# Sample attention over cached rows: block turns on VectorE, contractions of 32 on 16 tiles of TensorE, rotary keys loaded as stored

## The reference

```python
def sample_attention(q_lat, q_rope, c_kv, k_rope, cache_ckv, cache_krope, page_table):
    ...                                # m0, l0, acc0 from the new tokens
    def step(carry, pages):
        m, l, acc = carry
        ck = cache_ckv[pages]          # 128 rows x 256
        kr = cache_krope[pages]        # 128 rows x 64
        s = mla_scores(q_lat, q_rope, ck, kr)      # q_lat.ck + q_rope.kr
        m_new = jnp.maximum(m, jnp.max(s, axis=-1))
        alpha = jnp.exp(m - m_new)
        p = jnp.exp(s - m_new[..., None])
        l = l * alpha + jnp.sum(p, axis=-1)
        acc = acc * alpha[..., None] + jnp.einsum('bhqk,bkc->bqhc', p, ck, ...)
        return (m_new, l, acc), None
```

## Time and profile before

| | us | share of the span |
|---|---|---|
| span | 1993.0 | |
| TensorE matmuls (PE) | 1818.9 | 91% |
| TensorE weight loads (PEld) | 1240.8 | 62% |
| VectorE (DVE) | 751.0 | 38% |
| ScalarE (ACT) | 453.6 | 23% |
| GpSimd (POOL) | 318.3 | 16% |

### The profile page before, as it was taken

The page is one execution under the profiler, slowest core; times in us unless marked ns, Lnnn a source line. Parts: engine busy times, 40 slices in busy tenths (PEclk is TensorE's granted clock), DMA queues, the critical chain, the costliest instruction groups (busy, mean ns, idle before and its releaser), DMA issues.

```text
span 1993.0 us, 28968 instructions
## 1 busy us (share of the span) xinstructions
PE 1818.9 (91%) x11420; PEld 1240.8 (62%) x11420; DVE 751.0 (38%) x1684; ACT 453.6 (23%) x999; POOL 318.3 (16%) x437
## 2 busy tenths in 40 slices
PE   7999999999979999999999997999698888898884
PEld 5677888888845655656666664655465565565551
DVE  3343334444423434334554554576322311111116
ACT  3122211111113323223443443222110101111013
POOL 1034311111110000001111112333411211111100
PEclk9999999999989999999999997999698998998997
DMA  6112215555620000027999984545699999999986
GB/s 209 56 66 76 76 56 212 211 213 212 223 86 1 1 1 1 1 64 219 308 293 301 306 292 173 184 137 179 255 415 415 417 415 406 413 397 396 415 326 262
DMA packets 107021, 432.89 MB, mean 217 GB/s; under 512 B 25216, under 2 KB 30752, under 8 KB 77184
## 3 DMA queue, kind: packets, MB, share of 16 engines
q1 hardware_dynamic: 86704, 330.02, 44.2%
q0 software_dynamic: 20160, 101.24, 14.8%
q10 hardware_dynamic: 48, 0.13, 0.0%
HBM read 388.12 MB, written 63.66 MB: 227 GB/s over the span
## 4 chain that ended last, share of the span: by engine, by line
PE 33%; DMA 17%; DVE 2%; issue 1%; SPq 1%; ACT 1%; POOL 0%; POOLq 0%; DVEq 0%; ACTq 0%; PEldq 0%
DMA arena<-in_w_up_dram 16%; PE psum L1414 8%; PE psum L1158 6%; PE psum L1288 6%; PE psum L1169 4%; PE psum L1185 3%; PE psum L1271 1%; PE psum L1176 1%; SPq L802 1%; DMA arena<-in_w_down_dram 1%; PE psum L1313 1%; PE psum L1433 1%; DMA arena<-y_rows 0%; DVE arena L2547 0%; PE psum L1278 0%
## 5 line engine op out<-in xcount | busy, mean ns | idle before, releaser
L931 PE MATMUL psum<-arena 128*128 128x256 f32 x1792 | 394.0, 380 | 2.0 <-DVE arena L2116 2.0
L931 PEld LDWEIGHTS psum<-arena 128*128 128x128 f32 x1792 | 338.7, 190 | 55.7 <-issue 5.4
L1414 PE MATMUL psum<-arena 128*64 128x256 f32 (+1 forms) x2048 | 286.8, 414 | 65.7 <-DMA arena<-in_w_up_dram 63.9
L1414 PEld LDWEIGHTS psum<-arena 128*64 128x64 f32 (+1 forms) x2048 | 203.3, 156 | 139.3 <-issue 80.1
L2494 DVE TENSOR_TENSOR arena<-arena,psum 128x256 f32<-128x256 f32 x36 | 15.2, 423 | 314.4 <-ACT arena L1716 314.4
L1433 PE MATMUL psum<-arena 128*64 128x512 f32 (+1 forms) x512 | 131.3, 595 | 2.7 <-DMA arena<-in_w_down_dram 2.7
L1158 PEld LDWEIGHTS psum<-arena 128*128 128x128 f32 x1024 | 113.7, 142 | 29.5 <-issue 27.9
L1158 PE MATMUL psum<-arena 128*128 128x128 f32 x1024 | 127.3, 277 | 0.0
L1288 PE MATMUL psum<-arena 128*128 128x512 f32 x256 | 115.2, 603 | 1.3 <-ACT arena L1649 1.3
L1614 ACT COPY arena<-psum 128x512 f32<-128x512 f32 x128 | 72.0, 588 | 171.6 <-PE psum L1158 171.6
L1931 POOL DMA_INDIRECT y_rows<-arena x36 | 40.4, 1123 | 407.3 <-DVE arena L2503 407.3
(11 more groups left out here) (337 smaller groups left out, 2273.0 us busy)
## 6 DMA issues: line engine op xcount, KB each, us to landing
arena<-in_w_gate_dram SPq DMA_DIRECT2D x64, 1024.0 KB, 11.8
arena<-in_w_up_dram SPq DMA_DIRECT2D x64, 1024.0 KB, 20.2
arena<-in_w_down_dram SPq DMA_DIRECT2D x64, 1024.0 KB, 22.0
arena<-in_w_in_dram SPq DMA_DIRECT2D x8, 2048.0 KB, 10.9
z_act<-arena SPq DMA_DIRECT2D x64, 256.0 KB, 2.1
rope_turned<-arena SPq DMA_DIRECT2D x32, 512.0 KB, 4.8
arena<-rope_turned SPq DMA_DIRECT2D x64, 256.0 KB, 9.1
arena<-z_act SPq DMA_DIRECT2D x8, 2048.0 KB, 7.9
```

The lines of the kernel that those rows point to most:

```text
L931: last = mm(out[:, 0:256], x[:, k, :], w[:, k, :], start=(k == 0), stop=(k == 3))
L1414: last = mm(bank(2 + u)[rows, DE * x:DE * x + DE], xg_t[u][:, k, rows], w_e[slot][x][:, k, :], start=(k == 0), stop=(k == KD - 1))
```

## The change

VectorE turns each chunk as it lies, in blocks of 32x32, with two instructions of 128x2048 (turn_keys), straight from ck[q] into a flat tile ck_f; TensorE's turns, their copies on ScalarE and VectorE and the tile ck_t are gone. A block of 32 partitions of ck_f then holds 32 of the 256 latent values of the rows of its own 32 partitions, so the score contracts over 32 at a time: ten steps (eight latent, two rotary), for four row tiles a and four column tiles j, 160 calls with 128 columns each. Row tile a writes bank a; the scores of a chunk lie in four banks, a quarter of each, two chunks side by side. The queries are spread to all four groups of partitions by 24 small DMAs during the attention of the prompt (q_rep, qr_rep) and copied for each sequence on VectorE. The rotary keys are read with one DMA of 512 KB in pieces of 4 KB, as they lie in rope_turned, into two places; the load for n waits for the score of n - 2.

VectorE's round for chunk n: maximum, its two small steps, the additions of chunk n - 1 (in the last chunk of four those of chunk n too, at the end), the turns of chunk n + 2. In the last round of four the copies of the next queries stand ahead of the maximum. Chunk 0 is turned within the last units of the prompt's attention, chunk 1 ahead of the loop. TensorE's order: turn_probs n, score n + 1, weigh n. The loads of z wait for the weighing of chunk 29, w_o for that of chunk 30 (before: z for 28 and 29, w_o for 30 and 31).

```diff
             def rope_load(n):
-                if n >= 4:
-                    sp.wait_ge(c_s, n - 3)
-                sp.wait_ge(rk_mv[n % 2], 16 * PRE + 32 * (n // 2))
-                keys = rope_t[P * n:P * n + P, :].rearrange("(a f) (c m) -> c f a m", a=4, c=2)
-                for c in range(2):
-                    sp.dma_start(rope_home(n)[32 * c:32 * c + 32, :].rearrange("f (a m) -> f a m", a=4),
-                                 keys[c]).then_inc(rk_mv[n % 2], 16)
+                if n >= 2:
+                    sp.wait_ge(c_s, n - 1)
+                sp.wait_ge(rk_mv[n % 2], 16 * PRE + 16 * (n // 2))
+                sp.dma_start(kr_f[n % 2].rearrange("p c m -> p (c m)"), rope_t[P * n:P * n + P, :]).then_inc(rk_mv[n % 2], 16)
...
+            rope_load(0)
+            for u in range(2):
+                sp.wait_ge(b_ev[u], groups_done(sched, ("sL", 3))[u])
+            for a in range(4):
+                rows = slice(32 * a, 32 * a + 32)
+                for f in range(4):
+                    sp.dma_start(q_rep[rows, :, f, :], qs[32 * f:32 * f + 32, :, :]).then_inc(qrep_in, 16)
+                for f in range(2):
+                    sp.dma_start(qr_rep[rows, f, :], qsr[32 * f:32 * f + 32, :]).then_inc(qrep_in, 16)
             sp.wait_ge(ends, 8)
+            rope_load(1)
...
+            def score(n, q):
+
+                for f in (8, 9, *range(8)):
+                    for a in range(4):
+                        rows = slice(32 * a, 32 * a + 32)
+                        for j in range(4):
+                            keys = kr_f[q % 2][rows, f - 8, P * j:P * j + P] if f >= 8 else ck_f[q % 2][f // 4][rows, f % 4, 4 * j:4 * j + 4, :]
+                            last = mm(scores_at(q)[RS * j:RS * j + RS, a, :], q_now[rows, f, :], keys, start=(f == 8), stop=(f == 7))
                 last.then_inc(c_s, 1)
...
                     if more:
-                        pe.wait_ge(c_in[(q + 1) % 4], 16 * i + (16 if q < 3 else 32) + (16 * PRE if (q + 1) % 4 < 2 else 0))
-                        turn(n + 1, (q + 1) % 4, range(6))
+                        score_inputs(n + 1, (q + 1) % 4, 2 * i + (q + 1) // 2 + 1)
+                        if q == 3:
+                            pe.wait_ge(q_ready, i + 2)
                     turn_probs(n)
                     if more:
-                        turn(n + 1, (q + 1) % 4, range(6, NU))
+                        score(n + 1, (q + 1) % 4)
                     weigh(n, q)
-                    if more:
-                        if q == 3:
-                            pe.wait_ge(q_ready, i + 2)
-                        score(n + 1, (q + 1) % 4, 2 * i + (q + 1) // 2 + 1)
...
+            def turn_keys(q, half):
+                V.transpose(ck_f[q % 2][half].rearrange("p f r i -> p r f i"),
+                            ck[q][:, :, P * half:P * half + P].rearrange("p r (f k) -> p r f k", f=4)).then_inc(c_tr, 1)
+
             for what, n in late_units:
                 unit(what, n)
+                if (what, n) in (("PV", NTP * H // 2 - 3), ("PV", NTP * H // 2 - 2)):
+                    dve.wait_ge(c_in[0], 16 * PRE + 16)
+                    turn_keys(0, n - NTP * H // 2 + 3)
...
                     dve.wait_ge(c_s, n + 1)
-                    ch(red(m_part, bank(5), AX.X, ALU.max))
+                    if q == 3 and not last_batch:
+
+                        now = bass.ds(RS * i + RS, RS)
+                        for c in range(2):
+                            ts(q_now[:, 4 * c:4 * c + 4, :], q_rep[:, c, :, now], 1.0, None, ALU.mult)
+                        ts(q_now[:, 8:10, :], qr_rep[:, :, now], 1.0, None, ALU.mult).then_inc(q_ready, 1)
+                    ch(red(m_part, scores_at(q), AX.XY, ALU.max))
...
+                    if q:
+                        add_chunk(n - 1, (q - 1) % 2)
+                    if q < 2 or not last_batch:
+                        dve.wait_ge(c_in[(q + 2) % 4], 16 * i + (16 if q < 2 else 32) + (0 if q < 2 else 16 * PRE))
+                        for half in range(2):
+                            turn_keys((q + 2) % 4, half)
+                    if q == 3:
+                        if last_batch:
+                            dve.wait_ge(uv_in, 32)
+                            v_norm(0, 0)
+                        add_chunk(n, 1)
```

More of the change, by code:

```diff
@@ L1148, in _, with score_inputs @@
             last.then_inc(n_pe, 1)
[L1149 to L1170 removed]
+            def score_inputs(n, q, loads):
+                pe.wait_ge(rk_mv[q % 2], 16 * PRE + 16 * loads)
+                pe.wait_ge(c_tr, 2 * n + 2)
+            def score(n, q):
[5 more added lines that the diff above has]
+                            last = mm(scores_at(q)[RS * j:RS * j + RS, a, :], q_now[rows, f, :], keys, start=(f == 8), stop=(f == 7))
                 last.then_inc(c_s, 1)
@@ L1187, in weigh @@
                 last.then_inc(c_pv, 1)
-            pe.wait_ge(c_in[0], 16 * PRE + 16)
-            turn(0, 0, range(4), first=True)
+            pe.wait_ge(q_ready, 1)
+            score_inputs(0, 0, 1)
+            score(0, 0)
             pe.wait_ge(n_act, 1)
@@ L1194, in _ @@
             last.then_inc(n_pe, 1)
-            turn(0, 0, range(4, 6))
             pe.wait_ge(n_dve, 2)
@@ L1200, in _ @@
             last.then_inc(n_pe, 1)
-            turn(0, 0, range(6, NU))
             pe.wait_ge(n_dve, 3)
-            pe.wait_ge(q_ready, 1)
-            score(0, 0, 1)
             def batch(i, last_batch):
@@ L1608, in _ @@
             stage_end(act, 2)
-            def turned(n, us):
-                for u in us:
-                    act.wait_ge(c_tr, NU * n + u + 1)
-                    nc.scalar.copy(turned_at(u), bank(u % 4)).then_inc(kt_in[0], 1)
-            turned(0, (0,))
             act.wait_ge(c_sub, 1)
             A(p_new[0:RS, :], s_new[0:RS, :], ACT.Exp, scale=SCALE).then_inc(n_act, 1)
-            turned(0, range(2, NU, 2))
             def batch(i, last_batch):
@@ L2172, in _ @@
             dve.sem_inc(n_dve, 1)
+            dve.wait_ge(qrep_in, 16 * 24)
+            for c in range(2):
+                copy(q_now[:, 4 * c:4 * c + 4, :], q_rep[:, c, :, 0:RS])
+            copy(q_now[:, 8:10, :], qr_rep[:, :, 0:RS]).then_inc(q_ready, 1)
             stage_end(dve, 2)
-            dve.wait_ge(n_dve, 1)
-            for c in range(2):
-                copy(q_now[:, c, :], qs[:, c, 0:RS])
-            copy(qr_now, qsr[:, 0:RS]).then_inc(q_ready, 1)
             dve.wait_ge(rows_stored, 16 * 12)
@@ L2189, in _ @@
             copy(m_now[:, 0:1], m_all[:, 0:1])
-            def turned(n, us):
-                for u in us:
-                    dve.wait_ge(c_tr, NU * n + u + 1)
-                    copy(turned_at(u), bank(u % 4)).then_inc(kt_in[1], 1)
-            turned(0, (1, 3))
             dve.wait_ge(n_act, 1)
@@ L2221, in batch, with add_chunk @@
                 acc_b, l_b, m_b = acc_flat[:, bass.ds(KVL * i, KVL)], l_all[:, bass.ds(i, 1)], m_all[:, bass.ds(i, 1)]
+                def add_chunk(n, u):
+                    dve.wait_ge(c_p, n + 1)
+                    ch(stt(l_b, l_b, alpha[u], l_add[u], ALU.mult, ALU.add))
+                    dve.wait_ge(c_pv, n + 1)
+                    ch(stt(acc_b, acc_b, alpha[u], bank(7)[:, 0:KVL], ALU.mult, ALU.add))
+                    dve.sem_inc(c_acc, 1)
                 for q in range(4):
                     n = 4 * i + q
-                    more = q < 3 or not last_batch
@@ L2227, in batch @@
                     ch(tt(m_now[:, q + 1:q + 2], m_now[:, q:q + 1], m_part, ALU.max))
                     ts(neg_m, m_now[:, q + 1:q + 2], -SCALE, None, ALU.mult).then_inc(c_neg, 1)
-                    if q == 3 and more:
-                        for c in range(2):
-                            ts(q_now[:, c, :], qs[:, c, bass.ds(RS * i + RS, RS)], 1.0, None, ALU.mult)
-                        ts(qr_now, qsr[:, bass.ds(RS * i + RS, RS)], 1.0, None, ALU.mult).then_inc(q_ready, 1)
-                    if more:
-                        turned(n + 1, range(1, NU, 2))
@@ L2236, in batch @@
-                    dve.wait_ge(c_p, n + 1)
-                    ch(stt(l_b, l_b, alpha, l_add, ALU.mult, ALU.add))
-                    if not more:
-                        dve.wait_ge(uv_in, 32)
-                        v_norm(0, 0)
-                    dve.wait_ge(c_pv, n + 1)
-                    ch(stt(acc_b, acc_b, alpha, bank(7)[:, 0:KVL], ALU.mult, ALU.add))
-                    dve.sem_inc(c_acc, 1)
+                    if q:
+                        add_chunk(n - 1, (q - 1) % 2)
+                    if q < 2 or not last_batch:
+                        dve.wait_ge(c_in[(q + 2) % 4], 16 * i + (16 if q < 2 else 32) + (0 if q < 2 else 16 * PRE))
+                        for half in range(2):
+                            turn_keys((q + 2) % 4, half)
```

79 lines of the change are left out of this document (27 added, 52 removed).

## The result

The changed kernel takes 2216.75 us (median of 4 runs, 2209.15 to 2217.47) against 1992.24 for the kernel before (median, with a fourth run of it): the ratio of the means is 1.1117, with a 95% interval of 1.1087 to 1.1147. I had forecast 2033 and a range up to 2070. The direction was right, and so was half of the mechanism (TensorE's code is brought again in every pass); the path by which that costs time was wrong, and the size, +224 us for a forecast +40, was far off.

What follows compares the result with a forecast made beforehand. TensorE was taken to bound sample attention, DMA engines close behind; afterwards refetched code loading one DMA engine, 10.3 us a chunk, gave +37, other terms +39 to +40: 2033 us from 1993.0, range 1945 to 2070 (forecast's own 1999 to 2063).

Steps and rivals of the forecast that it cites:

- What bounds the kernel before: In sample attention TensorE sets the pace, 8.74 us a chunk, 3.81 of it turns; DMA engines about 5% behind.
- How often the code comes: TensorE's loop body, 11.4 packets after the change, is brought again each pass: 2.85 packets a chunk.
- What the code costs: In sample attention each packet takes one DMA engine 1.1 us, 10.3 us a chunk with its other loads; TensorE's waits hide.
- The price of a pair: In the score, 320 pairs of 128 columns, all 16 tiles running at once: score 2.4 us with its tail.
- Rival 3: Slower: every score pair costs L1260's 25 ns; score 8.1 us, chain 11.0, +64, 2057 us; chance 0.09.
- rival 2: Slower or same: score long through half clock or L911's pair price; chain 9.2 us, about 2001 us; chance 0.16.
- VectorE: VectorE's round per chunk with two block turns of 2.29 us each: 6.5 us, average 7.2.
- The start: First score some 9 us earlier, buying nothing; chunk 0's turns hidden in late attention, at most +1 for the second.
- DMA: Per chunk in sample attention: rotary keys 1.3 us in one transfer, with gathers' 5.92 making 7.2 us.
- Rival 1: Faster: code fetches don't bind, because the loop stays or they spread; period 7.6 us, 1948 us; chance 0.27.
- ring: The gathers' ring of four buffers in sample attention: some 30 us for four chunks, 7.5 a chunk.

Runs made afterwards that it cites:

- ten slices held: Changed kernel with TensorE's inner loop of two chunks, weighing from one fixed w_uv tile, all ten score slices: 2039.86 us.
- three-slice kernel: Changed kernel with the score cut to three slices (two rotary, one latent): 1983.45 us.
- two-chunk loop: Changed kernel whole, TensorE's batch loop given an inner loop run twice over two chunks, weighing in two versions behind branches: 2192.91 us (ratio 1.1005).

## Why the prediction was wrong, step by step

**What bounds the kernel before.** Right as far as it was tested: TensorE's 3.8 us of turns were on the path, and the DMA engines stood just behind.

**How often the code comes.** Right. I had 160 packets (the terms as written, 71 and 8 x 11.4, make 162); it is 169: the program's 91 and 13 a pass instead of 11.4 for six repeated passes. A body of 5.6 packets stays, one of 7.2 doesn't, and one of 6.1 is there behind the outer branch and is brought again behind the inner one.

**What the code costs: the step that failed.** The prediction said that the packets would load one DMA engine, that gathers would wait for its sixteenth, and that "the waits of TensorE for a packet, behind a taken branch too, hide behind landings in this case". The first two agree with the records as far as they go. From 1068.50 to 1070.00 in the kernel after one packet of q8, 0.97 us long, is all that moves, and the DMA share is 0.04: 0.97 us of one engine in 16. Whether it is always the same engine no record shows. Of the 128 packets of a gather, most of which run side by side, the last three start one by one at 1021.08, 1021.69 and 1022.30, and VectorE goes on behind the last of all: with ten slices held they end at 1078.08, and its turns start at 1078.38. But the kernel before without its loop showed no such load (0.9998 where +9 us were due). In the kernel after the DMA share is 0.45 and q8 takes 1.3% of 16 engines from 1000 to 1200, which on one engine alone would be 21% of it; by an estimate from these two that engine stands at 0.65. Its gathers land 9.4 us after issue (median, for 10.5 before), and VectorE waits for none in those 200 us. The sentence on hiding is the wrong one: I had a packet's time on its queue (1.1 us) and took it for the time between asking and having. Packets that TensorE asks for one after another start 3.47 us apart in a calm stretch and about 6.5 under a gather, and in the kernel after no two of them overlap. The score goes through 2.5 packets, which at 13 ns a pair want 1.7 us each. The rows of before showed 18 packets in 400 us; none bore on what happens when TensorE wants one every 2 us, and I should have asked that. I bounded the packet's cost on the DMA side from below and above and on TensorE's side not at all; the term was 0, and is at least 6.3 us a chunk, 176 us. That the kernel got slower was forecast, then, but not for the reason that made it slower: with no DMA engine at its limit, the forecast's own path gives nothing of its +40.

**The price of a pair: mis-sized.** The prediction took 6.7 ns (all 16 tiles at once), with 18 as the bound from L911. Its rate for four tiles is in the records of the kernel before: the groups of four matmuls of 512 columns in L1169 start at 1092.576, 1093.005 and 1093.435, 0.43 us apart, and the four loads of a group 7 ns apart. That 16 tiles do four times as much was its estimate, and no run shows it. A pair is 13.2 at full clock and 19.8 at half (2.17 us less 0.27 for 96 pairs in the three-slice kernel). So the score with its code held is 4.4 to 6.05 us and not 2.4. Rival 3's 25 ns, taken from L1260, isn't the price of a pair here: 13.2. So its 8.1 us for the score were too long as well, and the pair lies between the forecast's price and L911's. The granted clock of 0.72 in the stage, half behind each long pause (128 pairs in 2.81 us at 1064.11) and full later (128 in 1.89 us at 1095.97), is what rival 2 described; it raised the score to 6.05 in one round of four even where the code stayed.

**VectorE.** The turn's price was right, 2.292 us for 2.29. The 0.96 columns a ns under it are in the trace of the kernel before: the reduces of L2047 take 291 ns for 128 columns and 1224 for 1024, 133 for each 128 more. Right was also its place in the late attention: both turns of chunk 0 lie in idle time (887.53 and 897.09, and the work behind them starts with 2.93 and 0.58 us to spare). The round was too short: 7.30 us from maximum to maximum (1066.47 to 1073.77 with ten slices held) for 6.5, because the two additions of chunk n - 1, with their wait of 0.84 for a weighing that TensorE does after the score, take 1.7 us and not 0.85. In the kernel after that wait is 3.4 us a chunk (41.0 in 12).

**The start.** The first score was to come 9 us earlier and buy nothing. It starts at 909.62 for 923.64, but the first maximum comes at 934.66 for 928.13: VectorE waits 7.12 us for the weighing of the new rows (L1194, 7.03 us, where L1198 took 3.63) and then turns chunk 1 (4.5) ahead of it. That cost stood in no sum.

**DMA.** The rotary keys cost 15.4% of the engines from 1000 to 1170 with ten slices held, 9.94 MB or 19 loads of 512 KB: 1.4 us a chunk, for 1.3. The two queues fill 0.76 of the engines there: the rounds wait for the landing of single gathers, not for engines that are full.

**Rival 1.** 7.6 us and 1948 had the code stayed: also wrong. Measured with the code staying it is 9.30 us in the loop (9.59 with the last batch's chunks), and +45 in all. It was built as the largest of three means (ring, DMA, VectorE); the rounds show that in each another one comes last, and that the sum of those is what one gets.

Not settled: what makes a pair cost 13.2 ns, since the order of tiles doesn't change it; and why a body of 6.1 packets is there behind the outer branch and brought again behind the inner one, in the one kernel with such a body. How much of the 45 us a rearranged batch end would give back wasn't tried. No version here beats the kernel before with all of the work done; those that took less time leave part of the score out.

## What to carry to other kernels

Before unrolling work into many small instructions, count the instructions of the loop body: a loop whose code stays costs nothing to fetch (here one of 1436 did: q8 brought 85 packets in the whole run and none from 1000 to 1200 us), one of 1834 was brought again in every pass, and TensorE then went through its code at 256 instructions in 3.5 us, 6.5 beside large gathers. Writing the loop out instead gained nothing (2216.07 us). A resource that is hardly used (q8 at 0.5% of the DMA engines) can still be the bound when its user gets one piece at a time: ask for its latency, not for its share. And where several engines have nearly equal means, work out each round by itself, because the period is the mean of the rounds' largest and not the largest of the means.

## What was not expected of the hardware

- Code comes to TensorE in packets of 16 KB, 3.47 us from start to start with about 1.0 us on the queue, and none of the kernel after overlaps another (in the two-chunk loop five do); beside a gather of 16 KB packets it is about 6.5 us (1076.79 to 1083.34). With 1 KB gather packets the stage's period fell from 15.9 to 13.4 us.
- Bodies of 3, 4.2, 5.2 and 5.6 packets were brought once, bodies of 7.2, 8.2 and 11.2 in each pass with nine, ten and thirteen packets. One of 6.1 with an inner branch was brought again in each second inner pass, with nine, and not in the first.
- Pairs of load and matmul on tiles of 32x32 with 128 columns are 13.2 ns apart at full clock and 19.8 at half, not twice as far; the order of the tiles changes neither (1.49 and 2.17 to 2.18 us for 96 pairs).
- A block turn of 128x2048 in float32 takes 2.292 us with a strided target, where the turn of 128x512 gave 2.29 for it: the stride added nothing that shows.
